# Dilated attention on one core: two residues of dilation 16 in a block, partial sums joined inside the block loop, no separate combination stage

## The reference

```python
# 6 heads of 64 channels; DILATED_PATTERNS = ((128, 1), (512, 4), (2048, 16)), SWA_BLOCK = 128
def dilated_attention(q, k, v):
    for window, dil in DILATED_PATTERNS:
        # tokens t, t-dil, ... t-window: each residue class of t mod dil is a sequence of its own,
        # in which a query sees the 128 keys before it (and itself), causally
        o, lse = banded_causal_attention(to_sub(q), to_sub(k), to_sub(v), window // dil)
    w = jax.nn.softmax(jnp.stack(lses, axis=0), axis=0)
    return jnp.einsum('pbsh,pbshd->bshd', w, jnp.stack(outs, axis=0))
...
o_c = rms_norm(o_c.astype(x.dtype).reshape(B, S, SWA_WIDTH), swa_norm[l])
```

## Time and profile before

| | us |
|---|---|
| median of 3 runs (lowest, highest) | 2747.89 (2747.3, 2752.16) |
| the profiled execution's own time | 2746.48 |
| its span in the trace | 2744.7 |
| PE, DVE, ACT, POOL busy in the span | 2497.3, 1630.1, 1112.5, 724.1 |

### The profile page before, as it was taken

How to read it: one execution, slowest core, us unless ns; L and a number is a source line. 1 busy time by engine, 2 the same in 40 slices (tenths; PEclk the granted TensorE clock), 3 DMA queues, 4 the chain that set the end, 5 groups by cost and what they waited for, 6 DMA issues and landing times.

```text
span 2744.7 us, 33259 instructions
## 1 busy us (share of the span) xinstructions
PE 2497.3 (91%) x12320; PEld 2011.5 (73%) x12320; DVE 1630.1 (59%) x2237; ACT 1112.5 (41%) x1884; POOL 724.1 (26%) x616
## 2 busy tenths in 40 slices
PE   7999999999599990599599999989989999998995
PEld 5777777777377770487488888878868888887884
DVE  7445457763255567436577777735567877763435
ACT  6442443331255561421454444423535444442332
POOL 4111014430113334032433333103124534320103
PEclk9999999999799995799799999999999999999997
DMA  4332234431400014635422212164622322214462
GB/s 153 112 99 98 82 120 147 150 121 59 179 31 28 31 43 151 239 127 186 185 82 80 88 74 92 62 226 163 240 92 94 129 85 77 92 62 158 169 241 107
DMA packets 147633, 326.31 MB, mean 119 GB/s; under 512 B 18432, under 2 KB 58384, under 8 KB 138256
## 3 DMA queue, kind: packets, MB, share of 16 engines
q1 hardware_dynamic: 147472, 324.18, 34.1%
HBM read 230.52 MB, written 93.62 MB: 118 GB/s over the span
## 4 chain that ended last, share of the span: by engine, by line
PE 44%; DVE 3%; ACT 1%; DMA 1%; issue 1%; POOL 1%; SPq 0%; DVEq 0%; ACTq 0%; POOLq 0%
PE ff_bank L1941 15%; PE ff_bank L1943 15%; PE ff_bank L1942 15%; DVE ff_y L2524 1%; POOL ffn_rstd L2268 1%; DMA ff_b_raw<-h_t 1%; DVE ff_x2d L2555 1%; DVE ffn_rstd L2551 0%; DMA ff_a_raw<-a_t 0%; ACT ff_y L2363 0%; ACT ff_b_hi L2326 0%; DVE ff_x2d L2546 0%; DVE ff_a_lo L2538 0%; DVE ff_ring L2486 0%; ACT ff_e L2354 0%
## 5 line engine op out<-in xcount | busy, mean ns | idle before, releaser
L1941 PE MATMUL ff_bank<-ff_b_hi,ff_ring 128*128 128x512 f32 x1232 | 483.9, 393 | 36.8 <-DVE ff_ring L2486 15.1
L1942 PE MATMUL ff_bank<-ff_b_lo,ff_ring 128*128 128x512 f32 x1232 | 482.3, 391 | 0.0
L1943 PE MATMUL ff_bank<-ff_b_hi,ff_ring 128*128 128x512 f32 x1232 | 481.9, 391 | 0.0
L66 PE MATMUL ip_bank<-ip_x_hi,ip_w_hi 128*128 128x512 f32 x736 | 307.2, 417 | 20.0 <-DVE ip_x_lo L701 16.8
L1941 PEld LDWEIGHTS ff_bank<-ff_b_hi,ff_ring 128*128 128x128 f32 x1232 | 233.0, 189 | 89.9 <-issue 31.4
L67 PE MATMUL ip_bank<-ip_x_lo,ip_w_hi 128*128 128x512 f32 x736 | 296.6, 403 | 0.0
L68 PE MATMUL ip_bank<-ip_x_hi,ip_w_lo 128*128 128x512 f32 x736 | 296.0, 402 | 0.0
L1941 PE MATMUL ff_bank<-ff_a_hi,ff_w_hi 128*128 128x512 f32 x704 | 276.6, 393 | 15.9 <-DVE ff_a_lo L2538 15.8
L2524 DVE SCALAR_TENSOR_TENSOR ff_y<-ff_u,ff_conv_all,ff_y 128x1024 f32<-128x1024 f32 x176 | 240.2, 1365 | 63.4 <-ACT ff_y L2363 60.2
L1942 PE MATMUL ff_bank<-ff_a_lo,ff_w_hi 128*128 128x512 f32 x704 | 275.5, 391 | 0.0
L1943 PE MATMUL ff_bank<-ff_a_hi,ff_w_lo 128*128 128x512 f32 x704 | 275.3, 391 | 0.0
(11 more groups left out here) (245 smaller groups left out, 4623.6 us busy)
## 6 DMA issues: line engine op xcount, KB each, us to landing
ff_raw<-in_slabs SPq DMA_DIRECT2D x44, 1024.0 KB, 4.8
ff_a_raw<-a_t SPq DMA_DIRECT2D x88, 512.0 KB, 4.0
proj_t<-ip_staged SPq DMA_DIRECT2D x92, 256.0 KB, 2.7
a_t<-ff_y SPq DMA_DIRECT2D x44, 512.0 KB, 2.7
ff_w_raw<-in_w_down SPq DMA_DIRECT2D x88, 256.0 KB, 2.7
rp_tables<-in_rope SPq DMA_DIRECT2D x24, 512.0 KB, 4.4
ip_w_raw<-in_w_in SPq DMA_DIRECT2D x23, 512.0 KB, 4.0
o_scratch<-at_o_sb SPq DMA_DIRECT2D x48, 198.0 KB, 1.9
```

The costliest lines, as they stand in the source:

```text
L66: pe.matmul(out, w_hi[k], x_hi[k], start=(k == 0), stop=False)
L1941: pe.matmul(out, w_hi, x_hi, start=first, stop=False, skip_group_check=resumed)
L1942: pe.matmul(out, w_hi, x_lo, start=False, stop=False, skip_group_check=resumed)
L1943: return pe.matmul(out, w_lo, x_hi, start=False, stop=last, skip_group_check=resumed)
```

## The change

The 48 blocks become 40 turns in another order: 16 tiles at dilation 1, 8 double turns at dilation 16, 16 tiles at dilation 4. A double turn holds two residues, each with its own query and key tile, in the place of the two key tiles of a wide block.

- At dilation 1 nothing is staged: PE reads queries, keys and values straight from `at_qkv`. The turned values stay in a ring of eight tiles and are also stored to a new `v_scratch`; the later turns load their values from there, with tokens on the partitions, so neither POOL nor PE handles values there.
- The masks are three of 256 columns. Q, K and V are loaded in four blocks of 512 tokens, and the first turns wait for the first block.
- From turn 16 on, the sums of the tokens so far are loaded back (`at_rows`) and joined: DVE finds the lower of the two negated maxima (`find_low`), POOL takes two differences (`log_weights`), ACT their exponentials (`weights`), DVE weighs the new sums on the way out of PSUM (`take_sums`), and, in the turn that follows, POOL weighs the loaded ones (`weigh`) and adds (`join`). After a double turn the joined sums are stored again.
- At dilation 4, the last pattern, the joined sums are final. DVE divides them (`normalise`), ACT takes the sum of squares, a logarithm and an exponential for the norm's factor (`norm`), POOL writes a diagonal matrix of it, and PE turns the tile by a matmul against that matrix (`turn_outputs`), three turns after its scores. ACT applies the gain, and SP stores blocks of four tiles.
- `patterns` is gone.

```diff
 def attention_blocks():
-    for pat, dil in enumerate(DILATIONS):
-        for r in range(dil):
-            for b in range(S // dil // SPAN):
-                yield pat, r, b
+    for b in range(TILES_0):
+        yield 0, 0, b
+    for r in range(DILATIONS[1]):
+        for b in range(2):
+            yield 2, r, b
+    for b in range(S // (DILATIONS[1] * SPAN)):
+        for r in range(DILATIONS[1]):
+            yield 1, r, b
...
         @block.gpsimd
+            for j in range(TILES_0 - 1, TURNS + 4):
+                if TILES_0 <= j - 2 < TURNS:
+                    weigh(j - 2)
+                    join(j - 2)
+                if j + 1 < TURNS:
+                    stage(j + 1)
+                if FIRST_1 <= j - 3 < TURNS:
+                    make_diagonal(j - 3)
+                if TILES_0 <= j - 1 < TURNS:
+                    log_weights(j - 1)
...
         @block.scalar
+            def norm(i):
+                f = i - FIRST_1
...
+                act.activation(squares[:, :], o_f[:, i % 2, :], ACT.Square, accum_out=ss[:, i % 2, :]).then_inc(squared, 1)
+                act.wait_ge(squared, f + 1)
+                act.activation(ss[:, i % 2, :], ss[:, i % 2, :], ACT.Ln, bias=eps[:, :], scale=1.0 / CW).then_inc(ln_ready, 1)
+                act.wait_ge(ln_ready, f + 1)
+                act.activation(ss[:, i % 2, :], ss[:, i % 2, :], ACT.Exp, scale=-0.5).then_inc(rstd_ready, 1)
...
+            for j in range(TURNS + 5):
+                if j < TURNS:
+                    exps(j, 0)
+                    exps(j, 1)
+                if 0 <= j - 1 < TURNS:
+                    turned_odd(j - 1)
+                if j < TURNS:
+                    exps(j, 2)
+                if TILES_0 <= j - 1 < TURNS:
+                    weights(j - 1)
+                if j < TILES_0:
+                    take_values(j)
+                if TILES_0 <= j + 1 < FIRST_1:
+                    stage_queries(j + 1)
+                if FIRST_1 <= j - 4 < TURNS:
+                    take_outputs(j - 4)
+                if FIRST_1 <= j - 2 < TURNS:
+                    norm(j - 2)
...
         @block.vector
+            def take_sums(i):
+                dve.wait_ge(o_done, i + 1)
...
+                    dve.wait_ge(weight_ready, i - TILES_0 + 1)
...
+                    dve.tensor_tensor(per_head(sums_at(i)), per_head(o_pair[:, 0:parts(i), 0:NEG]), weight_of(i, 0), ALU.mult).then_inc(o_taken, 1)
...
         @block.tensor
+            def turn_outputs(i):
+                f = i - FIRST_1
+                pe.wait_ge(diagonal_ready, f + 1)
...
+                for g in range(GROUPS):
+                    ins = pe.matmul(v_bank[:, g * SPAN:(g + 1) * SPAN], o_f[:, i % 2, g * SPAN:(g + 1) * SPAN], diagonal[:, i % 2, :],
+                                    start=True, stop=True)
```

More of the change, by code:

```diff
@@ L1176, in dilated_attention, with blk, double, tokens @@
         blocks = list(attention_blocks())
+        def blk(b):
+            return slice(b * NB, (b + 1) * NB)
+        def double(j):
+            return TILES_0 <= j < FIRST_1
+        def tokens(a, j):
+            pat, r, b = blocks[j]
+            at = qkv[:, a, :, :]
+            if pat == 2:
+                return at.rearrange("p g (i c q) -> p g q c i", c=4, q=4)[:, :, r, 2 * b:2 * b + 2, :]
+            dil = DILATIONS[pat]
+            first = dil * SPAN * b + r
+            return at[:, :, first:first + dil * (SPAN - 1) + 1:dil]
@@ new lines, in parts, with scores_at, per_head, weight_of @@
+        def parts(j):
+            return 2 if double(j) else 1
+        def scores_at(j, g):
+            return s_pair[(GROUPS * j + g) % 2][:, :, 0:2 * SPAN]
+        def per_head(x):
+            return x.rearrange("p c (h d) -> p c h d", d=OW)
+        def weight_of(i, which):
+            return weight[:, i % 2, which, 0:parts(i), :].unsqueeze(3).to_broadcast([P, parts(i), HEADS, OW])
+        def sums_at(i):
+            return o_sb[:, i % 2, 0:parts(i), 0:NEG]
+        def rows_at(i):
+            return rows[:, (i - TILES_0) % R_RING, 0:parts(i), 0:NEG]
@@ new lines, in load_rows @@
+            def load_rows(j):
+                m = j - TILES_0
+                if j < FIRST_1:
+                    for p in range(2):
+                        sp.wait_ge(stored[p], 16 * TILES_0 // 2)
+                else:
+                    needed = TILES_0 + 2 * (blocks[j][1] + 1)
+                    for p in range(2):
+                        sp.wait_ge(stored[p], 16 * needed // 2)
+                if m >= R_RING:
+                    sp.wait_ge(joined, m - R_RING + 1)
+                sp.dma_start(rows[:, m % R_RING, 0:parts(j), :], rows_of(o_scratch[0 if j < FIRST_1 else 1], j)).then_inc(rows_in[m % R_RING], 16)
@@ L1183, in _, with store_out @@
+            def store_out(b):
+                sp.wait_ge(out_ready, 4 * (b + 1))
+                sp.dma_start(mix_t[5:8, :, blk(b)].rearrange("g p s -> p g s"), out[:, b % 2, :, :]).then_inc(out_stored[b % 2], 16)
+            load_qkv(0)
             sp.dma_start(idb[:, :], ident_bf).then_inc(consts_in, 16)
             sp.dma_start(mask[:, :, :], masks).then_inc(consts_in, 16)
[L1185 to L1190, removed]
@@ L1191, in _ @@
-            for p in range(2):
[L1192 to L1200, removed]
+            sp.dma_start(idf[:, :], ident).then_inc(consts_in, 16)
+            sp.dma_start(gain[:, :], swa_gain).then_inc(gain_in, 16)
+            for b in range(1, BLOCKS):
+                load_qkv(b)
@@ new lines, in _ @@
+            for j in range(TURNS):
+                if j < TILES_0:
+                    store_values(j)
+                if j == TILES_0 - 1:
+                    load_values(TILES_0)
+                if j == TILES_0:
+                    load_values(j + 1)
+                if 1 <= j <= TILES_0:
+                    store_sums(j - 1)
+                if j == TILES_0:
+                    load_rows(j)
+                    load_rows(j + 1)
+                if TILES_0 <= j and j + 2 < TURNS:
+                    load_values(j + 2)
+                if TILES_0 <= j - 2 < FIRST_1:
+                    store_sums(j - 2)
+                if TILES_0 <= j and j + 2 < TURNS:
+                    load_rows(j + 2)
+                if j >= FIRST_1 + 8 and (j - FIRST_1) % 4 == 0:
+                    store_out((j - FIRST_1) // 4 - 2)
@@ L1255, in take_values @@
[L1255 to L1269, removed]
-                for g in range(GROUPS):
[L1271 to L1276, removed]
@@ L1291, in turned_even @@
[L1291 to L1304, removed]
@@ L1306, in start @@
[L1306 to L1317, removed]
-                turned_even(j - 1, 1 - slot, wide, 0, last_fresh)
-                maxima(j, slot, wide, 1)
-                turned_even(j - 1, 1 - slot, wide, 2, last_fresh)
-                maxima(j, slot, wide, 2)
-                take_sums(j - 1, 1 - slot, uses)
@@ new lines, in _ @@
+            for j in range(TURNS + 2):
+                if j < TURNS:
+                    maxima(j, 0)
+                if 0 <= j - 1 < TURNS:
+                    turned_even(j - 1, 0)
+                if j < TURNS:
+                    maxima(j, 1)
+                if FIRST_1 <= j - 2:
+                    normalise(j - 2)
+                if 0 <= j - 1 < TURNS:
+                    turned_even(j - 1, 2)
+                if j < TURNS:
+                    maxima(j, 2)
+                if TILES_0 <= j - 1 < TURNS:
+                    find_low(j - 1)
+                if 0 <= j - 1 < TURNS:
+                    take_sums(j - 1)
@@ L1358, in scores @@
                 if GROUPS * j + g >= 2:
                     pe.wait_ge(probs_ready, GROUPS * j + g - 1)
-                at = mask[:, j, :] if wide else mask[:, 1, SPAN:]
-                out = scores_at(j, g, width)
+                at = mask[:, 2 if double(j) else 1 if b else 0, :]
+                to = scores_at(j, g)
                 for hh in range(2):
-                    pe.matmul(out[:, hh, :], idb[:, :], at, start=True, stop=False)
-                for hh in range(2):
-                    rows = slice(HD * hh, HD * (hh + 1))
-                    ins = pe.matmul(out[:, hh, :], q_s[rows, slot, g, :], k_s[rows, slot, g, 0:width], start=False, stop=True)
+                    pe.matmul(to[:, hh, :], idb[:, :], at, start=True, stop=False)
@@ new lines, in scores @@
+                n = 2 * SPAN // parts(j)
+                for c in range(parts(j)):
+                    for hh in range(2):
+                        heads = slice(HD * hh, HD * (hh + 1))
+                        if pat == 0:
+                            q = qkv[heads, 0, g, b * SPAN:(b + 1) * SPAN]
+                            k = qkv[heads, 1, g, max(b - 1, 0) * SPAN:max(b + 1, 2) * SPAN]
+                        else:
+                            q = q_s[heads, j % 2, g, c * SPAN:(c + 1) * SPAN]
+                            k = k_s[heads, j % 2, g, n * c:n * (c + 1)]
```

(35 more changed lines are left out.)

564 lines of the change are left out of this document (285 added, 279 removed).

## The result

The changed kernel takes 2705.3 us in the median (2703.9 to 2707.3, 4 runs) beside 2747.6 for the kernel before: ratio 0.9846, 95% interval 0.9829 to 0.9863, so 42 us faster where 104 were forecast. The profiled execution took 2707.28 us, its span is 2705.5. In the profiles the attention, from its first load to the next stage's, takes 390.3 us where it took 434.1, and the stages behind it, whose code is the same, 1628.4 us where they took 1623.5.

What follows compares the result with a forecast made beforehand. PE was taken to bound the wide blocks; 11.0 + 15.0 + 101.1 + 59.9 + 120.6 + 16.3 + 6 = 329.9 us of attention against 434.1 gave 2644 us, range 2630 to 2675.

Steps and rivals of the forecast that it cites:

- my sum: The attention from its first load to the next stage's, added piece by piece: 329.9 us against 434.1.
- my range: Kernel time, 8 in 10: 2630 to 2675 us; the likeliest case's own range 2630 to 2658.
- the waits that I had put in: What other engines do to PE in 24 turns: 6 us, lower end 0.
- Start, dilation 1, tail: Attention's start 11.0 us, sixteen turns at dilation 1 at 15.0 plus 101.1, its end through the last store 16.3.
- PE's work per turn: PE's time in the later turns: 7.49 us per double turn, 7.54 per turn at dilation 4.
- What hides the joining: Later turns: each ends no earlier than PE's last sums; loop 3.1 us, 4.2 in double turns, fits PE's 5.1.
- third rival: In the 24 later turns, joining comes in series with PE, 126 us in place of 6: 2764 us; chance 0.03.
- first rival: POOL and the port shared with DVE set the pace of the 24 later turns: 2663 us; chance 0.26.
- second rival: Reloading isn't in time at turn 16: a stall of 6 to 10 us, once or twice, 2652 us; chance 0.07.
- A sign that came true: Stages behind the attention: the forecast is wrong if a later one moves by over 3 us.

Runs made afterwards that it cites:

- both moves: Against the kernel after: double-turn queries staged two turns ahead, and turned outputs taken before the last exponentials; 2632.9 us, ratio 0.9594.

## Why the prediction was wrong

The direction was right and the size wrong: 42 us for 104. The attention's span from first load to the next stage's is 434.1 us before, 390.3 after, 319.6 with both moves, and 329.9 in my sum. That both moves, at 2632.9 us, end inside my range doesn't make the sum right for them: 6 of the 10 us between 329.9 and 319.6 are the waits that I had put in. I had also charged the output matmuls to sixteen turns; the first three have none, and theirs fall behind the last turn. Term by term:

| | forecast | after | with both moves |
|---|---|---|---|
| first load to first matmul | 11.0 | 9.9 | 9.8 |
| a turn at dilation 1 | 7.22 | 7.22 | 7.22 |
| a double turn | 7.49 | 10.29 | 6.98 |
| a turn at dilation 4 with outputs | 7.54 | 11.19 | 7.61 |
| from the last taking of sums to the next stage | 11.3 | 12.6 | 12.5 |

- *Start, dilation 1, tail:* right within 1.3 us.
- *PE's work per turn:* right for dilation 4, with 0.72 for the output matmuls where I took 0.65. Too high for the double turns: eight records of 128 columns took 0.65 (852.43 to 853.08), as long as four of 256 in the earlier trace rows, where I had scaled the 0.42 of four from the earlier trace rows. By 0.5 us in eight turns I overstated them by 4 us.
- *What hides the joining: this step failed.* I compared each engine's sum with a turn's length, and followed only the loop through the weights. I wrote that ACT's staging of 1.6 us fits into a double turn, not that it stands last in ACT's turn while the next turn's scores need it first. And I wrote for the third rival that "the waits point one to three turns back, so no such ring closes inside a turn". Two rings do: last scores, maxima, exponentials, weights, staging, next scores; and last scores, maxima, exponentials, weights, emptying the bank, output matmuls, last sums. The kernel before staged two blocks ahead. It did empty a single bank in its loop, that of the turned values (L1259), and also behind the last exponentials; but PE wrote that bank again only near the end of the next block. The changed kernel turns an output in the same turn in which the one before it is taken. Undoing the two positions, and nothing else, gave 70.8 us of the attention's span back, and 72 in the median.
- *The clock was missing from the sum altogether.* At dilation 4 a wait of 1.9 us cost 3.6 on average, since half clock followed it in most turns. I had put 6 us for all waits; with the half clock behind them they cost about 71.
- *The first rival (POOL and the port), 0.26:* wrong here. Its form, a slower turn, came true by another cause. POOL's products of 780 elements took 1.49 us, not the 2.21 of the earlier trace rows; DVE's division took 559 ns in the median and 761 at most; the weighing with one input in PSUM took 0.97 throughout. In the stage before, both engines did long products of two SBUF inputs side by side; here DVE's are short. What the Trainium skill (SBUF — State Buffer, "SBUF: two separate sides") says of the lock agrees with POOL's query copy beside the division, 1.27 us at 940.69 against 0.88 for its like elsewhere, but it set no turn.
- *The second rival (reloading):* small where the queries came in time: one turn of 7.8 to 8.5 in place of 7 at the first reload, 1.5 us at most. With both moves DVE's lower maximum waited 1.4 us there for the loaded rows.
- *The third rival (in series):* half right in kind. It looked for a ring through weigh, join and norm, which are indeed two turns apart, and not for one through staging and a single bank.
- *A sign that came true and means little:* I called the forecast wrong if a later stage moved by over 3 us. The output projection went from 207.4 to 210.5, but with the same code it lies between 204.1 and 211.3 over the experiments.

Beside the kernel with both moves, the kernel after loses 22 us in seven double turns (3.3 each in the steady ones; the reload lengthens the first to 8.11 in the kernel with both moves), 1.4 in the turn before them, 43 in the twelve at dilation 4 (3.6 each), and 5.0 in the last half turn (10.20 for 5.21): 71.6 together, against 70.8 by which its attention is longer.

## What to carry to other kernels

A busy sum below the turn's length proves nothing: for each instruction that an engine runs last in a turn, ask who needs it first in the next, and place both in time. A buffer that exists once, here a PSUM bank, closes a ring within the turn if it is emptied behind the turn's last exponentials and filled again in the same turn, even where every tile is handed on three turns behind. The same bank cost nothing at dilation 1, where it is emptied a turn ahead of its next use. On PE, a wait is to be priced with the half clock that can follow it, here 1.7 us behind 1.9 of waiting. What took both waits away was the order of ACT's instructions, not less work.

## What the runs showed of the hardware

- PE stood for 1.59 us in each double turn and for 1.72 us in each of the twelve turns with outputs, and was otherwise full. The granted clock was 0.84 and 0.81 over these stretches, and 0.54 to 0.55, close to the lower level (1.2 of 2.4 GHz), in the two places read behind a wait. It stayed at 1.00 where the same gap held 1.11 us of small matmuls and 0.77 us of standing still.
- The turns with outputs of the kernel after don't repeat. Four in a row took 9.51, 10.98, 11.78 and 12.02 us, with PE idle for 1.72 us in each; their granted clocks were 1.00, 0.85, 0.79 and 0.78.
- Products of two SBUF inputs on POOL took 1.49 us for 780 elements with DVE reading PSUM beside it, 2.21 in the median with DVE's long SBUF products beside it.
- Eight 32-bit records with 64 rows and 128 columns cost as much as four with 256 columns, 0.65 us.
